# Asking two ring slots earlier for what the second expert pass reads back from DRAM

## What is computed

```python
def chunk(args):
    hx, idx, g = args
    a = jax.nn.gelu(jnp.einsum("ced,cd->ce", u_emb[idx], hx), approximate=False)
    return jnp.einsum("ce,ced->cd", g * a, v_emb[idx])
```

## Time and profile before

| | us |
|---|---|
| median of three runs | 3646.63 |
| lowest, highest | 3644.4, 3656.96 |
| the profiled execution | 3649.95 |
| its span in the trace | 3647.9 |
| TensorE busy in it | 3485.0 (96%) |
| VectorE, ScalarE, GpSimd busy | 2196.4, 1245.6, 933.1 |
| from slot 3's to slot 123's start in the second pass | 687.94 |

### The profile page before, as it was taken

The page is one execution under the profiler, slowest core; times in us unless marked ns, Lnnn a source line. Parts: engine busy times, 40 slices in busy tenths (PEclk is TensorE's granted clock), DMA queues, the critical chain, the costliest instruction groups (busy, mean ns, idle before and its releaser), DMA issues.

```text
span 3647.9 us, 42986 instructions
## 1 busy us (share of the span) xinstructions
PE 3485.0 (96%) x16556; PEld 2811.5 (77%) x16556; DVE 2196.4 (60%) x3100; ACT 1245.6 (34%) x1821; POOL 933.1 (26%) x390
## 2 busy tenths in 40 slices
PE   7999898999999999999999999999899999999998
PEld 5777676887888888777777777888667888788885
DVE  6889846887888887455555556320358766542204
ACT  3234533222333333222222224332243656233223
POOL 0000143442000000344444444444202000344441
PEclk9999999999999999999999999999999999999999
DMA  3211132333446546555554552222212222322222
GB/s 107 93 53 41 58 110 98 122 122 121 164 164 210 168 168 208 196 185 185 185 184 184 183 185 90 94 98 97 96 63 81 70 79 73 110 94 97 98 87 81
DMA packets 144344, 446.75 MB, mean 122 GB/s; under 512 B 12761, under 2 KB 45913, under 8 KB 139921
## 3 DMA queue, kind: packets, MB, share of 16 engines
q1 hardware_dynamic: 108288, 405.26, 32.3%
q10 hardware_dynamic: 35856, 38.75, 3.1%
HBM read 372.64 MB, written 71.32 MB: 122 GB/s over the span
## 4 chain that ended last, share of the span: by engine, by line
PE 75%; DVE 11%; DMA 6%; DVEq 2%; issue 2%; ACT 2%; SPq 1%; POOL 0%; ACTq 0%; POOLq 0%
PE ps L212 51%; PE ps L997 10%; PE ps L1244 6%; DMA ring<-in_stream 6%; DVE conv_out L725 3%; PE ps L983 2%; DVE gated_lo L1184 2%; DVEq L718 1%; PE ps L231 1%; DVE m_gates L1939 1%; PE ps L1498 1%; PE ps L1442 1%; ACT gated_hi L1039 1%; DVE stats L784 1%; DVE norm_r L300 1%
## 5 line engine op out<-in xcount | busy, mean ns | idle before, releaser
L212 PE MATMUL ps<-h_norm_hi,slot_parts 128*128 128x512 f32 x4752 | 1528.6, 398 | 49.9 <-POOL slot_parts L200 14.5
L200 POOL TENSOR_TENSOR slot_parts<-ring,slot_parts 128x1024 fp32r<-128x1024 f32 x373 | 916.2, 2460 | 2373.1 <-ACT slot_parts L196 2373.0
L212 PEld LDWEIGHTS ps<-h_norm_hi,slot_parts 128*128 128x128 f32 x4752 | 898.5, 189 | 261.5 <-POOL slot_parts L200 24.6
L196 ACT ACTIVATE slot_parts<-ring 128x1024 fp32r<-128x1024 f32 x558 | 588.3, 1055 | 1028.1 <-DMA ring<-in_stream 832.0
L212 PE MATMUL ps<-x_low,slot_parts 128*128 128x512 f32 x2312 | 903.7, 391 | 0.0
L997 PE MATMUL ps<-gated_hi,slot_parts 128*128 128x512 f32 x2048 | 642.1, 392 | 38.7 <-DVE gated_lo L1184 38.7
L212 PEld LDWEIGHTS ps<-x_low,slot_parts 128*128 128x128 f32 x2312 | 438.6, 190 | 92.7 <-issue 1.9
L997 PEld LDWEIGHTS ps<-gated_hi,slot_parts 128*128 128x128 f32 x2048 | 386.3, 189 | 131.9 <-POOL slot_parts L200 52.1
L997 PE MATMUL ps<-gated_lo,slot_parts 128*128 128x512 f32 x1024 | 400.2, 391 | 0.0
L1184 DVE TENSOR_TENSOR gated_lo<-gated,gated_hi 128x512 fp32r<-128x512 f32 x128 | 252.5, 1973 | 203.3 <-ACT gated_hi L1039 195.4
L200 DVE TENSOR_TENSOR slot_parts<-ring,slot_parts 128x1024 fp32r<-128x1024 f32 x185 | 227.5, 1230 | 137.9 <-ACT slot_parts L196 133.1
(11 more groups left out here) (351 smaller groups left out, 3457.3 us busy)
## 6 DMA issues: line engine op xcount, KB each, us to landing
ring<-in_stream SPq DMA_DIRECT2D x560, 512.0 KB, 3.3
experts_dram<-experts SPq DMA_DIRECT2D x64, 512.0 KB, 4.7
gates_dram<-gates_by_key ACTq DMA_DIRECT2D x32, 1024.0 KB, 10.5
gates_back<-gates_dram SPq DMA_DIRECT2D x32, 1024.0 KB, 4.8
experts_back<-experts_dram SPq DMA_DIRECT2D x64, 512.0 KB, 4.7
x_res<-in_xT SPq DMA_DIRECT2D x2, 2048.0 KB, 9.7
x_dram<-x_res SPq DMA_DIRECT2D x4, 512.0 KB, 3.2
bias_by_distance<-bias_rows_dram ACTq DMA_DIRECT2D x8, 256.0 KB, 4.1
```

Source lines behind the costliest of these rows:

```text
L196: e.activation(to[:, BUFFER[n], 0, :], ring[:, n % RING, :], ACT.Copy).then_inc(s_hi, 1)
L200: e.tensor_tensor(to[:, BUFFER[n], 1, :], ring[:, n % RING, :], to[:, BUFFER[n], 0, :].bitcast(F32), ALU.subtract).then_inc(s_lo, 1)
L212: mm = e.matmul(psum, w2[wv][:, k, :], x2[xv], start=start and v == 0, stop=stop and v == 2)
```

## The change

peer_sp_back is called with n + 2 in place of n, in the turns from two before the second pass to two before its end. Each request for gates and experts, with the waits inside it, thus stands ahead of the request for ring slot j-2 in place of ring slot j. Nothing else differs: the orders of TensorE, VectorE, ScalarE and GpSimd are the same instruction by instruction.

```diff
-            if START["peer_v"] <= n < START["f1_in"]:
-                peer_sp_back(e, n - START["peer_v"])
+            if START["peer_v"] <= n + 2 < START["f1_in"]:
+                peer_sp_back(e, n + 2 - START["peer_v"])
             e.dma_start(ring[:, n % RING, :], a["stream"][n]).then_inc(arrive[n % RING], 16)
```

## The result

The change makes the kernel slower. The median of six runs is 3682.50 us (3677.65 to 3693.93), against 3649.61 for the kernel before beside it: the ratio is 1.0087, interval 1.0071 to 1.0103. The forecast was 3682 and 1.0% slower. The profiled execution is the quickest of the six (3677.65), and its span is 3675.6 us, 27.7 more than that of before (3647.9); the medians differ by 32.9.

The account below looks back on a forecast made before the run. TensorE was taken as the bound (75% of the chain), losing 1.1 us per four slots. A new two-slot loop, 59 x 12.07 us, gives +35.0, other terms 0: median 3682, 1.0% slower, range 3641 to 3698.

Parts of the forecast that it names:

- The largest wait: Second pass: VectorE waits 128.2 us in 30 pieces for experts_back; removing that wait gives nothing.
- The group's bytes: SP's queue: 1.5 MB stands ahead of ring slot 58, not 60; the 1.1 us per four slots only moves, cost 0.
- The new wait and its loop: SP's experts request waits for product n-1, ahead of ring slot n: 12.07 us per two slots against TensorE's 10.88.
- The loop's pieces: The two-slot loop through VectorE, SP, DMA and ScalarE: 2.80, 0.05, 5.11 and 4.11, sum 12.07 us.
- The gates' bytes: Turns with gates: their 1 MB moves during the product wait, taken at 0; uncovered, 1.9 us in 29 turns, +55.
- The start: First request, at ring slot -2, waits for the gates' writes to DRAM: 0 to +0.5 us, taken as 0.
- The sum: Slot 5 to slot 123: 59 loops x 12.07 = 712.1 us, slot 123 at 2228.4, not 2193.40: +35.0.
- The lower end of the forecast: Slower case's 3658: in a third of the loops the product is quick and TensorE's 10.88 counts, 24 off.
- That the stall only moves: Rival: VectorE's product is quick (0.68), the loop is 9.87, under 10.88, and hides; about 3647, chance 0.16.
- That the stall goes: Rival: ring slots come in time, slots 3 to 122 take 652.8 us, 35 off, about 3612; chance 0.08.
- More cost from the gates: Rival: the gates' bytes lie in the loop, +55 on top, about 3735; 0.03 of the chance for slower.
- the estimate was about +15: Skill's transfer figure put the pair of transfers at 4.8 us, the loop at 11.7; not used, 5.11 kept.

Follow-up runs that it names:

- three_buffers: Kernel after with a third experts_back buffer, so the request for pair j waits for the product of slot j-4, not j-3: 3656.83 us, ratio 1.0012.
- product_ahead: Kernel after with VectorE making product j+1 ahead of gated_lo j-1 in place of behind it: 3658.12 us, ratio 1.0015.
- shift_one: Kernel before with the gates and experts requests one slot ahead (n + 1), in place of the change's two: 3655.17 us, ratio 1.0005.
- hi_first_two: Kernel after with ScalarE's order changed in the second pass, gated_hi of slot j-1 ahead of the split of slot j: 3609.91 us, ratio 0.9882.

## Why the prediction was right, point by point

**The number.** The mechanism was right, and the size too: +35 in the sum, +31.5 in the trace over the same stretch, +32.9 between the medians. That 3682 meets 3682.50 to half a microsecond is luck. The forecast started from 3646.63, and the kernel before beside the result took 3649.61: the miss of 2.5 us in the difference (35.4 forecast, 32.9 measured) was made up by 3 us in the starting point.

**The largest wait.** The prediction calls VectorE's 128.2 us for experts_back the largest wait. Of the two lines of the earlier trace rows it is, but not in the whole view, where VectorE itself waits longer for gated_hi. Nothing in the sum hangs on it:

```profile
DVE gated_lo L1184 <- ACT gated_hi L1039: 181.2, 88, 2.9
```

**The group's bytes (0).** Right. Where the loop is open (three_buffers, product_ahead, shift_one) the 30 stalls and the time of before are back, and moving the gates alone changes nothing.

**The new wait and its loop.** Right in place and kind. The loop runs over SP, DMA, ScalarE and VectorE, over two slots; the slow products were forecast at about 60 with a mean near 1700 ns, and are 55 with 1625; TensorE's waits at about 60, and are 58; SP's wait for the product is there 56 times. That wait was put at 3.6 us, counted from when the slot is done, while the row's 333.9 us in 56 pieces, 6.0 each, takes in SP's idle time ahead of that: the two are not the same quantity, and I should have said which one the row shows.

**The loop's pieces.** For the turn with experts alone, from the end of gated_lo 53 (1800.48) and that with the gates ahead, from the end of gated_lo 55 (1812.53):

| piece | forecast | experts alone | behind gates |
|---|---|---|---|
| gated_lo's end to product's end | 2.80 | 2.82 | 2.81 |
| to SP's request | 0.05 | 0.08 | 0.08 |
| request to the split's start | 5.11 | 5.06 | 4.76 |
| split's start to gated_lo's end | 4.11 | 4.09 | 4.08 |
| sum | 12.07 | 12.05 | 11.73 |

The two splits that end the third piece:

```profile
1808.44 1.06 ACT L196 ACTIVATE slot_parts<-ring 128x1024 fp32r<-128x1024 f32 x1 [7.94 <-DMA ring<-in_stream]
...
1820.18 1.06 ACT L196 ACTIVATE slot_parts<-ring 128x1024 fp32r<-128x1024 f32 x1 [8.69 <-DMA ring<-in_stream]
```

**The gates' bytes (0, bound +55).** The value taken was right and a little too careful. (The bound was loosely worked out: the rows give 7.44 - 5.11 = 2.3 us for a turn, the prediction counts 1.9 without saying why, and 3682 + 55 is 3737, not 3735.) The gates are asked for at 1811.82, 3.60 us ahead of the experts at 1815.42, and the turn that has them is 0.3 us shorter than the one without, not longer:

```profile
1811.82 0.33 SPq L1067 DMA_DIRECT2D gates_back<-gates_dram  x1
1815.42 0.33 SPq L1072 DMA_DIRECT2D experts_back<-experts_dram  x1
1815.80 2.97 SPq L348 DMA_DIRECT2D ring<-in_stream  x2
```

**The start (0 to +0.5).** It took 0.47. SP got past its wait at 1455.20, right when the last gates' write had landed:

```profile
1442.27 12.86 DMA gates_dram<-gates_by_key
...
1455.20 0.33 SPq L1067
...
1456.05 7.70 DMA ring<-in_stream
```

All of this execution lies 4.67 us ahead there, so the write's end, 1455.13, is 1459.8 in the times of before: 1.2 us under the forecast's latest, 1461.0. The turn to the split of slot -2 (1463.83) then took 8.63 us in place of 7.44, 1.2 us more, so the split came where it was forecast (1468.5) by two misses that cancelled. The run with this edit alone shows no cost.

**The sum.** Forecast +35.0 from the start of the pass to slot 123, measured +31.5. The terms:
- from slot 0's start to the end of slot 2: 18.94 in place of 18.25, +0.7 (taken as the same). All of it lies in slot 0, 7.87 in place of 7.18, and there the granted clock was low for longer (0.83 over 1480 to 1500, 0.91 before);
- from there to slot 5's start: 11.86 in place of 11.7, +0.2;
- 59 loops: slot 5 starts at 1512.97 and slot 123 at 2220.67, 707.7 us or 11.995 each, in place of 12.07: -4.4.

The sum was thus 3.5 us too high, and the last term by 4.4. That is not the length of a closed loop: the loop did not hold throughout. Three times the slow products are 34.3 to 35.3 us apart in place of 36.2 for three loops (products 21 to 27, 49 to 55, 85 to 91). TensorE then runs four slots, once six, without a wait, and SP's next turn with gates starts the loop anew. These three places hold 9 of the 59 loops and took 104.0 us, 4.6 less than nine closed loops. The other 50 took 603.7, or 12.07 each, which is the forecast's figure. Why the loop opens just there is not shown. The lower end of the forecast had a third of the loops open; here it was three places.

That the 50 loops have the mean of 12.07 is in part luck again. It was worked out from one turn without gates, half of the turns have them, and in the table those are 0.3 us shorter. But most ring slots landed in 4.0 to 4.9 us, and in about one loop in eight in 5.1 to 5.9, for instance

```profile
1935.52 5.66 DMA ring<-in_stream
```

with 13.05 us to the next slow product there. In each of these seven loops one packet (8 or 16 KB) of a queue of the kind "instruction", as in the kernel with three buffers, began 0.6 to 1.0 us after the request for experts. No run takes these packets away, so that they delay the ring slot is not shown.

**The rivals.** That the stall only moves (3647) needed the product to be quick at nearly every turn; 43% are slow. But the experiments show it is what comes when the wait is met in time (1.0005 to 1.0015). That the stall goes (3612, a ratio of 0.990) is what comes when the ring slot is no longer behind the requests (0.9894 and 0.9899); the size was right and the condition was not met by this change. More cost from the gates (3735) did not come. By the figure of the Trainium skill ("DMA: Bandwidth & Descriptors", "Anatomy of one DMA") the estimate was about +15; the measured +31.5 lies by the sum from the row of this kernel, whose 5.11 us for the pair of transfers came back as 5.06 and 4.76. Only the turns behind the gates come near the 4.8 estimated from that page's figure.

## What to carry to other kernels

- A prefetch that is asked for earlier on an in-order queue takes its buffer-free wait along with it, and everything behind it waits too. Before moving it, ask which consumer frees its buffer, whether that is done at the new place, and what is queued behind; if the way from there back to that consumer closes a circle, add up the circle and compare it with the bound engine's work over the same distance.
- A large wait in a profile (here 128.2 us of VectorE for experts_back) may be worth nothing; follow the chain of one period to see what the bound engine waits for, and cut the link there. Here that was the order of two instructions, on SP or on ScalarE, at 1.0 to 1.3%.

## What the runs showed of the hardware

**Two transfers behind a running one are not slower.** With 1 MB of gates asked for 3.6 us earlier in the same queue and landing 4.66 us after its request, so still under way, the pair of experts and ring slot took 4.76 (and 4.73 at 1839.11) from request to split, without it 5.06 and 4.98.

**VectorE beside GpSimd.** The product of two float32 operands of 128x512 takes 0.68 us by itself and 2.88 when it starts while GpSimd makes two splits in a row, as these rows of the kernel after show. It then ends half a microsecond behind GpSimd's pair (1809.58 + 5.22 = 1814.80):

```profile
1812.46 2.88 DVE L1176 TENSOR_TENSOR gated<-gates_back,experts_back 128x512 f32<-128x512 f32 x1
...
1815.87 0.68 DVE L1176 TENSOR_TENSOR gated<-gates_back,experts_back 128x512 f32<-128x512 f32 x1
```

```profile
1809.58 5.22 POOL L200 TENSOR_TENSOR slot_parts<-ring,slot_parts 128x1024 fp32r<-128x1024 f32 x2 [6.83 <-ACT slot_parts L196]
```

In a closed loop this is 2.2 us of 12. Outside of one it cost nothing here: in hi_first_two 34 of 128 products are slow (mean 1265 ns), and four slots take 21.76 us, TensorE's own time, in every period from slot 3 to 123.

**TensorE's clock fell once between slots 3 and 123.** The window line of 1598 to 1602 (busy times, then PEclk): the granted clock there is 0.71 on average, some 2.3 of 4 us at 1.2 GHz in place of 2.4. Ahead of it TensorE had stood still for 1.82 us, up to 1598.79. But two longer stops, 1.91 us up to 1945.47 and 2.12 up to 2137.03, were followed by no fall, so the length of the stop alone does not tell. The clock returned while TensorE ran on without a wait. The fall cost about 1.7 us of the 31.5: the two slots from 1598.79 took 12.58 us in place of 10.88.

```profile
1598.00:1602.00 4.00, 3.21 (x10) 2.53 (x11) 4.00 (x4) 0.00 (x0) 2.88 (x2) 0.71 0.65 254
```

Over 1505 to 2190 the granted clock is 1.00 as before, so nearly all of the loss is waiting time and not clock.
